# A streaming encoder layer on one core: the order of query products, scores and values on TensorE in the attention stage

## Chip, cores and metric

The kernel runs on one core of one Trainium2 chip. The metric is the device time of one execution in microseconds (us); lower is better. Timed three times it gave 2192.12 us in the median (2192.0 to 2194.67).

## What is computed

Two layers of a hybrid encoder, each over 1024 prompt rows and 8 streams of 16 rows, so 1152 rows in all (9 tiles of 128 rows; tile index 8 holds the streams). Per layer:

```
proj = rms_norm(x) @ w_in          # a, gc, gb | q (8 heads) | k, v (2 kv heads) | u, vg
y_conv = gb * conv3(gc * a)
q, k   = partial_rope(q), partial_rope(k)
p      = exp(s - m) / (sum(exp(s - m)) + exp(sink - m)),  s = q k^T / 8 over this chunk and the one before
y_attn = p v
y_gmlp = gelu(u) * (W_s layer_norm(gelu(vg)) + b)
mix    = [rms(y_conv), rms(y_attn), rms(y_gmlp)]
x      = x + mix @ w_out
x      = x + relu(rms_norm(x) @ w_ff1)^2 @ w_ff2
```

All of it is in float32. A chunk is 64 rows; in a tile of 128 prompt rows the first 64 see the chunk before and their own, the last 64 see the whole tile. The streams see the cached keys of 64 rows and their own 16.

## The kernel before

**Products.** A float32 product is made of three TensorE matmuls on split operands (high times high, high times low, low times high): `product`, lines 2131 to 2135, so "one product" below is three matmuls. `rows_by_cols` (L2140) makes the product of one tile of rows with 512 columns of weights over the given depth slices `ks`; with eight slices that is 24 matmuls. It can be called in pieces: `sum_of` says which slice starts and which ends the sum in the bank of `ps`. Weights come as units of 128x512; ScalarE rounds a unit to its high half and VectorE subtracts to get the low half (`split` on both engines).

**The attention stage.** Each engine's program is an order written out by hand, with semaphores between engines. Tile t goes through these steps:

- `rows_by_cols(..., t, U_Q, ...)` on TensorE: the queries of tile t into bank 0 of `ps` (bank 1 for index 1);
- `copy_q(t)` on ScalarE (L1168, instruction L1172): out of PSUM into `qn`, of which there is one; it also waits for the turn of t-1;
- `rotate` on VectorE (L1417, instructions L1423 to L1426): the rotary part;
- `q_turn(t)` on TensorE (L2231, instruction L2239): four 128x128 transposes into bank 2; `copy_qT(t)` on ScalarE (L1176, L1182, or L1187 for tile index 8) brings them to `qT`;
- `scores(t)` on TensorE (L2242, instructions L2259 to L2266; L2274 and L2275 for index 8) into banks 3 and 4; it waits for `copy_qT(t)` and for the exponentials of t-1, which read the same banks;
- `softmax_max(t)` on VectorE (L1483, L1489 to L1494), `exponentials(t)` on ScalarE (L1189, L1199 and L1201), `softmax_norm(t)` on VectorE (L1496, L1499 to L1501);
- `p_turn(t)` on TensorE (L2279, L2285) into banks 5 and 6; `turned_back(t)` on ScalarE (L1224, instructions L1230 and L1231) brings them to `pT` and signals `pT_done`;
- `values(t)` on TensorE (L2289, L2305, or L2311 for index 8) into bank 7; it waits for `pT_done` of t, for `value_rows(t)` on VectorE (`vmix`) and for the copy of t-1 out of bank 7;
- `mixed_high(t)`, `squares_of(t)` on ScalarE, `mixed_low(t)`, `square_sums(t)` on VectorE, and `group_sums(t)` on TensorE (L2315): the operand of the output projection and its sums of squares.

TensorE runs them as a pipeline over i = 0 to 8: `q_turn(i-1)`, queries of i, `scores(i-1)`, `values(i-3)`, `p_turn(i-2)`, `group_sums(i-4)`. ScalarE in step i runs `copy_q(i)`, `mixed_high(i-3)`, `exponentials(i-1)`, `copy_qT(i)`, `squares_of(i-3)`, `turned_back(i-2)`; in the last step (i = 8) `copy_qT(8)` comes ahead of `exponentials(7)`, and four splits of output weights lie in between. So in ScalarE's order `turned_back(6)` stands behind `exponentials(7)` and `squares_of(5)`, and behind it come four splits, `exponentials(8)`, and then for tile indices 6 and 7 `mixed_high`, `squares_of` and the next `turned_back`.

**Behind the loop** TensorE drains the pipeline while the output projection begins: `side_rows(0, t)` (L2344) makes the columns 0 to 511 of the convolution and gating part for tile t (two groups of six matmuls, in two banks), and `add_sides(0, t)` on VectorE (L1546, instruction L1543) adds both groups to `x` and so frees the banks. `side_rows(0, 1)` uses the banks of `side_rows(0, 0)` and waits for them.

**Ahead of the loop** the queries of tile index 0 and the first half of those of index 1 are already made between convolution blocks. All of it runs once in each of the two layers.

Of the kernel before, what the change touches and what calls it, by code (L numbers as in the profile page):

```python
# [46 lines left out]
TS = T - 1  # L47
ROWS = T * P
KD = D // P
# [12 lines left out]
U_KVG, U_U, U_CONV, U_Q, U_OUT, U_FF, U_END = 0, 8, 12, 24, 32, 48, 60  # L62
# [69 lines left out]
def program(nc, io, plan):  # L132
# [5 lines left out]
    with ExitStack() as ctx:  # L138
# [125 lines left out]
        ps = ctx.enter_context(nc.psum_tensor("ps", [P, 8, 512], F32))  # L264
# [82 lines left out]
        def tile(t):  # L347
            return slice(t * P, (t + 1) * P)
# [1023 lines left out]
        def _(dve):  # L1372
# [143 lines left out]
            def mixed_low(t):  # L1516
                dve.wait_ge(*mix_hi.at(t))
                for k0, k1, src in ((0, 2, yc[:, :, tile(t)]), (2, 6, yat[:]),
                                    (6, 8, ygT[:, :, tile(t)])):
                    last = V.tensor_tensor(hTl[:, k0:k1, tile(t)], src, hTh[:, k0:k1, tile(t)].bitcast(F32),  # L1520
                                           ALU.subtract)
                last.then_inc(*mix_lo.tick(t))
# [23 lines left out]
            def add_sides(n, t):  # L1546
                add_rows(n, t, 0)
                add_rows(n, t, 2)
# [257 lines left out]
            for l in range(DEPTH):  # L1806
# [42 lines left out]
                for t in range(T + LAG[l]):  # L1849
# [14 lines left out]
                    i = t - LAG[l]  # L1864
# [46 lines left out]
                for i in range(T):  # L1911
                    if i == TS:
                        split(range(U_OUT, U_OUT + 2))
                    dve.wait_ge(*qn_raw.at(i))
                    rotate(qn[:], HEADS, i, q_rot)
                    if i >= 1:
                        softmax_max(i - 1)
                    if i == TS:
                        split(range(U_OUT + 2, U_OUT + 4))
                    if i >= 2:  # L1920
                        value_rows(i - 2)
                    if i >= 3:
                        mixed_low(i - 3)
                    if i >= 1:
                        softmax_norm(i - 1)
                    if i >= 4 and i < TS:
                        group_scale(i - 4)
                    if i >= 3 and i < TS:
                        square_sums(i - 3)

                add_sides(0, 0)
                softmax_max(TS)
                group_scale(TS - 4)
                square_sums(TS - 3)
# [195 lines left out]
        def _(pe):  # L2130
# [9 lines left out]
            def rows_by_cols(out, t, first_id, ks, cols=512, sum_of=None, at=None):  # L2140

                sum_of = sum_of or ks
                for n, k in enumerate(ks):
                    i = first_id + (k if at is None else at + n)
                    if t == 0:
                        unit_ready(i)
                    s = i % 8
                    ins = product(out, hTh[:, k, tile(t)], hTl[:, k, tile(t)], wh[:, s, 0:cols], wl[:, s, 0:cols],  # L2150
                                  k == sum_of[0], k == sum_of[-1])
                    if t == TS:
                        ins.then_inc(w_used.sem, 1)
                return ins
# [87 lines left out]
            def scores(t):  # L2242


                pe.wait_ge(*qT_done.at(t))
                if t >= 1:
                    pe.wait_ge(*exp_done.at(t - 1))
                else:
                    pe.wait_ge(*kc_done.at(None))
                    pe.wait_ge(*yc_done.at((1, 2)))  # L2250
                pe.nop(nofuse=True)
                k0 = t * P
                for h in range(G4):
                    if t == TS:
                        break
                    c0 = h * P
                    sides = [(ps[:, 3 + g, :], slice(64 * g, 64 * g + 64)) for g in range(2)]
                    for bank, rows in sides:
                        pe.matmul(bank[0:64, c0:c0 + 64], qT[rows, c0:c0 + 64], kT[rows, k0:k0 + 64], start=True,  # L2259
                                  stop=True)  # L2260
                    for bank, rows in sides:
                        ins = pe.matmul(bank[64:128, c0:c0 + P], qT[rows, c0 + 64:c0 + P], kT[rows, k0:k0 + P],  # L2262
                                        start=True, stop=True)
                    if t > 0:
                        for bank, rows in sides:
                            ins = pe.matmul(bank[0:64, c0 + 64:c0 + P], qT[rows, c0:c0 + 64], kT[rows, k0 - 64:k0],  # L2266
                                            start=True, stop=True)
                if t == TS:
                    for b in range(DEC_BATCH):
                        bank = ps[:, 3 + b // 4, (b % 4) * KEYS_S:(b % 4 + 1) * KEYS_S]  # L2270
                        for g in range(2):
                            rows = slice(64 * g, 64 * g + 64)
                            qb = qT[rows, b * 64:(b + 1) * 64]
                            pe.matmul(bank[rows, 0:64], qb, kcT[rows, b * 64:(b + 1) * 64], start=True, stop=True)  # L2274
                            ins = pe.matmul(bank[rows, 64:80], qb, kT[rows, k0 + 16 * b:k0 + 16 * b + 16],  # L2275
                                            start=True, stop=True)
                ins.then_inc(*sc_full.tick(t))
# [11 lines left out]
            def values(t):  # L2289

                pe.wait_ge(*pT_done.at(t))
                if t < TS:
                    pe.wait_ge(*vmix_set.at(t))
                if t >= 1:
                    pe.wait_ge(*yat_done.at(t - 1))
                else:
                    pe.wait_ge(*zst_out.at(1))
                out = ps[:, 7, :].rearrange("p (h n) -> p h n", h=G4)
                pv = pT[:].rearrange("p (g h n) -> p g h n", g=2, h=G4)
                if t < TS:  # L2300
                    for g in range(2):
                        rows = slice(64 * g, 64 * g + 64)
                        for half, vv in enumerate((vmix[:, rows], v_sb[:, t, rows])):
                            q = slice(64 * half, 64 * half + 64)
                            ins = pe.matmul(out[rows, :, q], vv, pv[:, g, :, q], start=True, stop=True)  # L2305
                else:
                    pe.wait_ge(*vs_in.at("last"))
                    for b in range(DEC_BATCH):
                        for g in range(2):
                            rows = slice(64 * g, 64 * g + 64)  # L2310
                            ins = pe.matmul(out[rows, :, 16 * b:16 * b + 16], vs[0:KEYS_S, b, rows],  # L2311
                                            pT[0:KEYS_S, b * P + 64 * g:b * P + 64 * g + 64], start=True, stop=True)
                ins.then_inc(*pv_full.tick(t))
# [30 lines left out]
            def side_rows(n, t):  # L2344
                if n == 0:
                    pe.wait_ge(*mix_lo.at(t))
                for part, (grp, ks) in enumerate(((0, (0, 1)), (2, (6, 7)))):
                    ins = rows_by_cols(out_bank(n, t, grp), t, U_OUT + 8 * n, ks, at=2 * part)
                    if t < TS:
                        ins.then_inc(*out_full.tick((n, t, grp)))  # L2350
# [132 lines left out]
            for l in range(DEPTH):  # L2483
# [8 lines left out]
                for t in range(T + LAG[l]):  # L2492
# [15 lines left out]
                    i = t - LAG[l]  # L2508
# [46 lines left out]
                pe.wait_ge(*z_done.at((1, 1)))  # L2555
                rows_by_cols(ps[:, 1, :], 1, U_Q, range(0, 4), sum_of=range(KD))
                rows_by_cols(ps[:, 0, :], 0, U_Q, range(6, KD), sum_of=range(KD)).then_inc(*q_full.tick(0))

                for i in range(T):
                    if i >= 1:  # L2560
                        q_turn(i - 1)
                        if i >= 2:
                            pe.wait_ge(*qn_raw.at(i - 1))
                        ins = rows_by_cols(ps[:, 1 if i == 1 else 0, :], i, U_Q,
                                           list(range(KD) if i >= 2 else range(KD // 2, KD)), sum_of=range(KD))
                        if i < TS:
                            ins.then_inc(*q_full.tick(i))
                        scores(i - 1)
                    if i >= 3:
                        values(i - 3)  # L2570
                    if i >= 2:
                        p_turn(i - 2)
                    if i >= 4:
                        group_sums(i - 4)


                q_turn(TS)
                side_rows(0, 0)
                scores(TS)
                side_rows(0, 1)  # L2580
                values(TS - 2)
                p_turn(TS - 1)
                group_sums(TS - 3)
                side_rows(0, 2)
# [91 lines left out]
```

## Time and profile before

| what | value |
| --- | --- |
| median of 3 runs | 2192.12 us (2192.0 to 2194.67) |
| the profiled execution | 2193.26 us |
| its span, first to last instruction | 2191.5 us |
| TensorE busy | 2158.0 us (98%) |
| VectorE busy | 1548.0 us (71%) |
| ScalarE busy | 937.3 us (43%) |
| mean granted clock of TensorE | 0.998 of full |
| chain that ended last | PE 93%, DVE 2%, ACT 2% |

The table is of one profiled execution, but for the first line. 1.8 us of its time lie around the span. "Granted clock" is the share of 2.4 GHz that TensorE was given. PE is TensorE's matmuls, PEld its weight loads, DVE is VectorE, ACT is ScalarE. Starts are counted from the span's start. In layer 0 the attention stage lies between 194 and 305 us, in layer 1 between 1278 and 1389 us.

### The profile page before, as it was taken

What the parts mean: (1) busy time and instruction counts of PE and PEld (TensorE: products, weight loads), DVE (VectorE), ACT (ScalarE), POOL (GpSimd) and SP (SyncE); (2) the same over time, 40 slices, a digit from 0 to 9 for tenths busy, and PEclk for the clock granted to TensorE, in tenths of its full rate; (3) what the DMA queues carried; (4) which work ended last, traced back from release to release, by engine and by line L of the source; (5) the groups of instructions that cost most, each with busy time, mean ns of one, the idle gap of its engine ahead of it and who ended that gap; (6) DMA issues with size and microseconds to landing.
All of it is one profiled execution on the core that took longest, in us unless ns stands there. A gap on an engine that the chain in (4) does not pass through costs nothing.

```text
span 2191.5 us, 34116 instructions
## 1 busy us (share of the span) xinstructions
PE 2158.0 (98%) x13154; PEld 1932.4 (88%) x13154; DVE 1548.0 (71%) x2597; ACT 937.3 (43%) x1951; POOL 111.6 (5%) x205
## 2 busy tenths in 40 slices
PE   7999999999999999999999999999999999999998
PEld 5898778999999988888879987889999998888886
DVE  5524767888787787777873348578878787877768
ACT  4313833555555523233342148235555555223233
POOL 2300011000000000000022000010000000000002
PEclk9999999999999999999999999999999999999999
DMA  5211012345555786536312100223454558856363
GB/s 169 61 42 34 21 49 96 125 157 209 195 191 185 283 303 254 212 137 230 99 45 66 46 19 21 70 104 140 169 210 176 197 188 338 299 179 230 137 228 116
DMA packets 218002, 330.35 MB, mean 151 GB/s; under 512 B 14172, under 2 KB 104576, under 8 KB 217840
## 3 DMA queue, kind: packets, MB, share of 16 engines
q1 hardware_dynamic: 214768, 321.93, 41.3%
q10 hardware_dynamic: 1008, 3.67, 0.4%
q0 software_dynamic: 2064, 2.57, 0.4%
q8 instruction: 105, 1.72, 0.3%
q14 instruction: 57, 0.47, 0.1%
HBM read 212.28 MB, written 115.64 MB: 150 GB/s over the span
## 4 chain that ended last, share of the span: by engine, by line
PE 93%; DVE 2%; ACT 2%; DMA 1%; issue 1%; POOL 0%; SPq 0%; DVEq 0%; ACTq 0%; POOLq 0%
PE ps L2133 30%; PE ps L2135 29%; PE ps L2134 29%; PE ps L2177 1%; DMA w_raw<-in_w_in 1%; PE ps L2305 1%; PE ps L2285 1%; DMA ff_ops<-row_op 1%; PE ps L2227 0%; ACT S L1199 0%; PE ps L2239 0%; DVE b_all L1561 0%; PE ps L2262 0%; PE ps L2259 0%; ACT q L927 0%
## 5 line engine op out<-in xcount | busy, mean ns | idle before, releaser
L2133 PE MATMUL ps<-h_all,w_hi 128*128 128x288 f32 (+1 forms) x1504 | 471.2, 313 | 0.9 <-DVE q L1695 0.9
L2135 PE MATMUL ps<-h_all,w_lo 128*128 128x288 f32 (+1 forms) x1504 | 470.2, 313 | 0.0
L2134 PE MATMUL ps<-h_all,w_hi 128*128 128x288 f32 (+1 forms) x1504 | 469.5, 312 | 0.0
L2133 PEld LDWEIGHTS ps<-h_all,w_hi 128*128 128x128 f32 x1504 | 282.2, 188 | 2.9 <-DVE q L1695 1.3
L2134 PEld LDWEIGHTS ps<-h_all,w_hi 128*128 128x128 f32 x1504 | 282.2, 188 | 0.1
L2135 PEld LDWEIGHTS ps<-h_all,w_lo 128*128 128x128 f32 x1504 | 282.2, 188 | 0.0
L2133 PE MATMUL ps<-w_hi,h_all 128*128 128x512 f32 x576 | 232.3, 403 | 2.9 <-DVE w_lo L1387 1.7
L2135 PE MATMUL ps<-w_hi,h_all 128*128 128x512 f32 x576 | 226.1, 393 | 0.0
L2134 PE MATMUL ps<-w_lo,h_all 128*128 128x512 f32 x576 | 226.0, 392 | 0.0
L2133 PE MATMUL ps<-w_hi,ring_all 128*128 128x512 f32 x544 | 211.6, 389 | 0.0
L2134 PE MATMUL ps<-w_lo,ring_all 128*128 128x512 f32 x544 | 211.6, 389 | 0.0
L2135 PE MATMUL ps<-w_hi,ring_all 128*128 128x512 f32 x544 | 211.6, 389 | 0.0
L2135 PE MATMUL ps<-s,w_lo 128*128 128x288 f32 x624 | 184.2, 295 | 0.0
L2134 PE MATMUL ps<-s,w_hi 128*128 128x288 f32 x624 | 183.7, 294 | 0.0
L2133 PE MATMUL ps<-s,w_hi 128*128 128x288 f32 x624 | 183.5, 294 | 0.0
L2133 PE MATMUL ps<-w_hi,ring 128*128 128x512 f32 x448 | 174.8, 390 | 0.3 <-DVE x L1781 0.3
L2135 PE MATMUL ps<-w_hi,ring 128*128 128x512 f32 x448 | 174.4, 389 | 0.0
L2134 PE MATMUL ps<-w_lo,ring 128*128 128x512 f32 x448 | 174.3, 389 | 0.0
L983 ACT ACTIVATE w_hi<-b_all 128x512 fp32r<-128x512 f32 x128 | 70.3, 621 | 237.6 <-PE ps L2135 174.1
L1006 ACT ACTIVATE w_hi<-w_raw 128x512 fp32r<-128x512 f32 x182 | 110.4, 624 | 111.7 <-DVE w_raw L1629 40.9
L983 ACT ACTIVATE w_hi<-w_raw 128x512 fp32r<-128x512 f32 x96 | 56.6, 629 | 186.9 <-DVE w_raw L1733 96.7
L2133 PEld LDWEIGHTS ps<-w_hi,h_all 128*128 128x128 f32 x576 | 109.1, 189 | 27.8 <-DVE w_lo L1387 3.2
(247 smaller groups left out, 4082.9 us busy)
## 6 DMA issues: line engine op xcount, KB each, us to landing
ff_ops<-row_op SPq DMA_DIRECT2D x128, 512.0 KB, 3.3
w_raw<-in_w_ff SPq DMA_DIRECT2D x128, 256.0 KB, 3.5
ring_all<-ff_ops SPq DMA_DIRECT2D x32, 1024.0 KB, 8.3
ring<-ff_ops SPq DMA_DIRECT2D x32, 1024.0 KB, 8.4
ff_raw<-q SPq DMA_DIRECT2D x96, 256.0 KB, 3.4
b_all<-in_w_ff SPq DMA_DIRECT2D x24, 1024.0 KB, 12.1
w_raw<-in_w_in SPq DMA_DIRECT2D x64, 256.0 KB, 3.4
ring<-ff_raw SPq DMA_DIRECT2D x12, 1024.0 KB, 5.6
```

The source lines that it names most:

```text
L983: nc.scalar.activation(wh[:, HALF * half + j, :], w[:, j, :], ACT.Copy).then_inc(op_hi, 1)
L1006: nc.scalar.activation(wh[:, fslot(b, i), :], raw[:, FRAW[kind], :], ACT.Copy).then_inc(f_hi, 1)
L2133: pe.matmul(out, sh, mh, start=first, stop=False)
L2134: pe.matmul(out, sh, ml, start=False, stop=False)
L2135: return pe.matmul(out, sl, mh, start=False, stop=last)
L2177: ins = pe.transpose(ps[:, bank, (k % 4) * P:(k % 4 + 1) * P], xn[:, t % 2, tile(k)], ident[:])
L2285: ins = pe.transpose(ps[0:n, 5 + h // 4, (h % 4) * P:(h % 4 + 1) * P], S[:, t % 2, h * n:(h + 1) * n], ident[:])
L2305: ins = pe.matmul(out[rows, :, q], vv, pv[:, g, :, q], start=True, stop=True)
```

## The change

On TensorE the second half of the queries of tile index 1 moves ahead of the loop, that is ahead of `q_turn(0)`. In step i = 1 there are then two of the eight depth slices of tile index 2 between `q_turn(0)` and `scores(0)`, and step i = 2 makes the other six. Behind the loop `values(6)` (`values(TS - 2)`, the seventh tile) moves from behind `side_rows(0, 1)` to ahead of `scores(8)`. On VectorE `add_sides(0, 0)` moves from behind the loop into step i = 8, ahead of `softmax_norm(7)`. ScalarE's order, the DMA queues and GpSimd are left as they are; no instruction is added or taken away.

```diff
@@ VectorE, in step i @@
                     if i >= 3:
                         mixed_low(i - 3)
+                    if i == TS:
+                        add_sides(0, 0)
                     if i >= 1:
                         softmax_norm(i - 1)
@@ VectorE, behind the loop @@
-                add_sides(0, 0)
                 softmax_max(TS)
@@ TensorE @@
                 rows_by_cols(ps[:, 0, :], 0, U_Q, range(6, KD), sum_of=range(KD)).then_inc(*q_full.tick(0))
+                rows_by_cols(ps[:, 1, :], 1, U_Q, range(4, KD), sum_of=range(KD)).then_inc(*q_full.tick(1))
 
                 for i in range(T):
                     if i >= 1:
                         q_turn(i - 1)
-                        if i >= 2:
-                            pe.wait_ge(*qn_raw.at(i - 1))
-                        ins = rows_by_cols(ps[:, 1 if i == 1 else 0, :], i, U_Q,
-                                           list(range(KD) if i >= 2 else range(KD // 2, KD)), sum_of=range(KD))
-                        if i < TS:
-                            ins.then_inc(*q_full.tick(i))
+                        if i == 1:
+                            pe.wait_ge(*qn_raw.at(0))
+                            rows_by_cols(ps[:, 0, :], 2, U_Q, range(0, 2), sum_of=range(KD))
+                        else:
+                            if i >= 3:
+                                pe.wait_ge(*qn_raw.at(i - 1))
+                            ins = rows_by_cols(ps[:, 0, :], i, U_Q, range(2 if i == 2 else 0, KD), sum_of=range(KD))
+                            if i < TS:
+                                ins.then_inc(*q_full.tick(i))
                         scores(i - 1)
@@ TensorE, behind the loop @@
                 q_turn(TS)
                 side_rows(0, 0)
+                values(TS - 2)
                 scores(TS)
                 side_rows(0, 1)
-                values(TS - 2)
                 p_turn(TS - 1)
```

## Rows read from the trace of the kernel before

**Rows 1.** The page: busy time, share of the span and instructions of each engine
```profile
PE 2158.0 (98%) x13154; PEld 1932.4 (88%) x13154; DVE 1548.0 (71%) x2597; ACT 937.3 (43%) x1951; POOL 111.6 (5%) x205
```

**Rows 2.** Waits of PE, whole span: total us, times, longest us
```profile
PE ps L2239 <- DVE qn L1426: 4.7, 4, 1.7
PE ps L2274 <- issue: 1.8, 2, 0.9
...
PE ps L2133 <- DVE x L1543: 0.7, 2, 0.4
```

**Rows 3.** Timeline of PE, layer 0, start of the loop: start us, us, idle before
```profile
193.80 0.39 PE L2135 MATMUL ps<-w_hi,h_all 128*128 128x512 f32 x1
195.87 0.66 PE L2239 MATMUL ps<-ident,qn 128*128 128x128 f32 x4 [1.68 <-DVE qn L1426]
196.28 0.48 PE L2133 MATMUL ps<-w_hi,h_all 128*128 128x512 f32 x1
...
199.21 0.27 PE L2259 MATMUL ps<-kT,qT 64*64 64x64 f32 x2
...
200.96 0.66 PE L2239 MATMUL ps<-ident,qn 128*128 128x128 f32 x4 [0.65 <-DVE qn L1426]
...
207.00 0.27 PE L2259 MATMUL ps<-kT,qT 64*64 64x64 f32 x2
...
208.09 1.09 PE L2285 MATMUL ps<-ident,S 128*128 128x128 f32 x8
```

**Rows 4.** Timeline of ACT, same stretch
```profile
196.56 0.60 ACT L1182 ACTIVATE qT<-ps 128x512 f32<-128x512 f32 x1 [1.74 <-PE ps L2239]
199.32 0.60 ACT L1172 ACTIVATE qn<-ps 128x512 f32<-128x512 f32 x1 [2.16 <-PE ps L2135]
...
206.18 0.64 ACT L1182 ACTIVATE qT<-ps 128x512 f32<-128x512 f32 x1
```

**Rows 5.** Timeline of DVE, same stretch
```profile
200.02 0.29 DVE L1423 TENSOR_TENSOR rtA<-qn,cosb 128x128 f32<-128x128 f32 x1 [4.21 <-ACT qn L1172]
...
200.61 0.29 DVE L1426 TENSOR_TENSOR qn<-rtA,rtB 128x128 f32<-128x128 f32 x1
201.08 0.48 DVE L1489 MEMSET ps<- 64x512 f32 x1 [0.17 <-DVE qn L1426]
...
206.80 1.22 DVE L1501 TENSOR_TENSOR S<-S,den 128x1024 f32<-128x1024 f32 x1
```

**Rows 6.** Timeline of PE, layer 0, behind the loop
```profile
269.12 0.39 PE L2135 MATMUL ps<-w_hi,h_all 128*128 128x512 f32 x1
270.40 0.34 PE L2274 MATMUL ps<-kcT,qT 64*64 64x64 f32 x4 [0.89 <-issue]
...
272.80 0.58 PE L2133 MATMUL ps<-w_hi,h_all 128*128 128x512 f32 x1 [0.35 <-DVE x L1543]
...
277.32 0.66 PE L2305 MATMUL ps<-pT,vmix 128*64 128x256 f32 x4
...
278.35 1.09 PE L2285 MATMUL ps<-ident,S 128*128 128x128 f32 x8
...
285.48 0.66 PE L2305 MATMUL ps<-pT,vmix 128*64 128x256 f32 x4
```

**Rows 7.** Timeline of ACT, same stretch
```profile
270.04 0.25 ACT L1201 ACTIVATE es<-sd 128x8 f32<-128x8 f32 x1
...
271.75 0.65 ACT L1231 ACTIVATE pT<-ps 128x512 f32<-128x512 f32 x1
...
281.71 0.59 ACT L1231 ACTIVATE pT<-ps 128x512 f32<-128x512 f32 x1
```

**Rows 8.** Timeline of DVE, same stretch: the sides of tile index 0
```profile
271.91 1.63 DVE L1543 SCALAR_TENSOR_TENSOR x<-ps,rG,x 128x512 f32<-128x512 f32 x2
```

**Rows 9.** Busy time in two stretches: PE, PEld, DVE, ACT, POOL (instructions), granted clock, DMA
```profile
272.80:277.32 4.52, 4.52 (x12) 3.31 (x12) 3.77 (x13) 4.52 (x21) 0.85 (x1) 0.62 0.00 0
1357.10:1360.00 2.90, 2.90 (x12) 2.14 (x12) 2.82 (x11) 2.90 (x11) 0.69 (x1) 1.00 0.00 0
```

## The prediction

> **What bounds the kernel now.** I read the page first: TensorE is busy for 98% of the span, VectorE for 71%, ScalarE for 43% [rows 1]. So no engine but TensorE matters on average, and a change that only reorders work can gain no more than the time in which TensorE stands still where the change is made. The table of waits says how much that is [rows 2]: TensorE waits four times for the rotated queries (4.7 us), twice ahead of the streams' scores (1.8 us) and twice for the banks of the first side products (0.7 us), 7.2 us in all over both layers. The timelines of layer 0 place them: 1.68 us ahead of the first turn, 0.65 us ahead of the second [rows 3], 0.89 and 0.35 us behind the loop [rows 6]. That makes 3.57 us in a layer, and layer 1 repeats it. All the rest of the stage has no gap on TensorE.
>
> The row of 0.89 us names "issue" as its releaser, which is to be read with care: `scores(8)` waits for the exponentials of index 7, and the last of these ends at 270.04 + 0.25 = 270.29 [rows 7], 0.11 us ahead of the start at 270.40 [rows 6]. I take 0.1 us as the way from ScalarE's end to TensorE's start below.
>
> **Part 1, the queries ahead.** Twelve matmuls of 512 columns move ahead of `q_turn(0)`, six of tile index 2 take their place. The pace of such matmuls comes from the timeline [rows 3]: the twelve between 196.28 and the scores at 199.21 took 2.93 us with the change to scores included; the 24 from 200.96 + 0.41 = 201.37 to 207.00 took 5.63, so twelve more cost 2.70 and one 0.225 us. (0.41 is the step from the turn at 195.87 to the next product at 196.28.)
>
> Now step by step, in times of layer 0. The last product ahead of the loop starts at 193.80 and hands over at 194.03. Twelve more end at 196.75; with 0.1 for the change of operand the first turn starts at 196.85. The queries are rotated well before that (the turn could start at 195.87), so the 1.68 us are filled. Products of index 2 start at 197.26; six take 2.93 - 6 x 0.225 = 1.58, so `scores(0)` starts at 198.84 instead of 199.21. Its `qT` copy moves with the turn from 196.56 to 197.54 and ends at 198.14 [rows 4], in time. Before, the scores ended at 200.96 - 0.65 = 200.31, 1.10 us after their start; now at 199.94. `copy_q(1)` needs the turn of index 0 and follows the `qT` copy in ScalarE's order: 198.14 to 198.74 instead of 199.32 to 199.92 [rows 4]; the rotation (200.02 to 200.90, so 0.98 us behind the copy) [rows 5] ends at 199.72. So `q_turn(1)` finds its data when `scores(0)` is through, at some 199.9, and the 0.65 us are filled too.
>
> **What is late next.** `softmax_max(0)` on VectorE starts when the scores are there, at 199.97 instead of 201.08 [rows 5]: 1.1 us earlier, and no more, since 0.4 us come from the scores and the rest from the rotation that no longer stands ahead of it. From there the chain is as before: maxima, eight exponentials, the `qT` copy of index 1 behind them in ScalarE's order (206.18, now 205.07, ending at 205.71) [rows 4], and `scores(1)`, which needs that copy. It was ready at 206.82, and TensorE came at 207.00 [rows 3]: nearly even. Now TensorE is through with the 18 remaining matmuls at 199.9 + 0.41 + (5.63 - 6 x 0.225) = 204.6, and can start at 205.8. A new wait of 1.2 us stands there. `p_turn(0)` needs the normalised S: 206.80 + 1.22 = 208.02 [rows 5], and ran at 208.09 [rows 3]; now 1.1 us earlier, right behind `scores(1)`. From there on everything is shifted by 1.1 us and nothing else. Gain of part 1: 1.1 us in a layer, not the 2.3 of the filled gaps. Bounds: no gain at all if another step of the first iterations proves tight, and 2.3.
>
> **Part 2, values ahead of the streams' scores.** `values(6)` needs `pT_done` of 6, that is `turned_back(6)` on ScalarE, which stands behind `exponentials(7)` and `squares_of(5)`. It ends at 271.75 + 0.65 = 272.40 [rows 7]. The side products end their issue at 269.12 + 0.23 = 269.35 [rows 6]. So TensorE would stand from there to 272.50, some 3 us, in place of the 0.89; ScalarE's program isn't changed and has no gap there, so `pT_done` doesn't come sooner against TensorE. Behind the waiting `values(6)` are queued `scores(8)`, whose own wait ends at 270.40, and everything after. The values take 278.35 - 277.32 = 1.03 us [rows 6], so `scores(8)` starts at 273.53; it takes 272.80 - 0.35 - 270.40 = 2.05, so `side_rows(0, 1)` starts at 275.58. Before, it started at 272.80 with the values still ahead of it, comparable to 273.83. Loss: 1.75 us in a layer. In the changed order the second gap (0.35) has gone, that is in this sum. Bounds: the loss can't be below 1.6 unless ScalarE is early, nor much above 2.
>
> Who waits for the later scores: `softmax_max(8)`, `exponentials(8)` start some 2.2 us later (the scores end at 275.58 instead of 272.45, ScalarE was still splitting weights). Behind them stands `turned_back(7)`, which ended at 281.71 + 0.59 = 282.30 against `values(7)` at 285.48 [rows 6, 7]: 3.2 us of cover, and TensorE comes later as well. I cost it at nothing; without this cover it would be up to 2 us.
>
> **Part 3, the adds.** Two instructions of 1.63 us together [rows 8] move ahead of `softmax_norm(7)`. They need side products that are out at 269.51 [rows 6] and free the banks before TensorE asks for them. `softmax_norm(7)` is then ready by some 273.2, and its reader `p_turn(7)` comes behind 278: nothing.
>
> **The clock.** Two stretches set side by side show one more thing [rows 9]: the twelve matmuls behind `scores(8)` took 4.52 us in layer 0, the same twelve 2.90 in layer 1. The granted clock was 0.62 in the mean of the first stretch and 1.00 in the second: TensorE had fallen to its lower level, 1.2 GHz, after the gap of 0.89, the small matmuls of the streams' scores and the gap of 0.35, and it cost 1.62 us. In layer 1 the same quiet stretch didn't bring it down. The change makes this stretch longer: 3.1 us standing, 1.03 of values, 2.05 of scores. I expect a fall in both layers more often than not, but part of the low clock then falls on the standing and on the scores, whose many small matmuls may be limited by their weight loads rather than by the array. The price per layer lies between 0 and 1.62 twice over; I take 1.0. The Trainium skill (TensorE: Matmul & The Clock Gate, Part 1) has the rule that the gate gives the full clock only to an engine kept busy and takes it back from a quiet one, and its advice is against gaps between bursts of matmuls. By that rule the change pays in both layers, which is rival (c) below with 2196.6; by the trace, one quiet stretch in two fell.
>
> **Sum.** Per layer -1.1 + 1.75 = +0.65, for both +1.3, and +2.0 for the clock. The profiled execution took 2193.26 us (span 2191.5 and 1.8 around it) and holds one fall of the clock for 1.62; without it it would be 2191.6. The median of the three runs, 2192.12, lies between, nearer to the one without a fall, and I count from it: 2192.1 + 1.3 + 2.0 = 2195.4. A difference under 0.2% (4.4 us) can't be told from none here, so this is no measurable change, on the slow side.
>
> **Rivals.** (a) All gaps go. For it: each edit lies at one of the four. It needs `turned_back(6)` ahead of 269.4 and the exponentials of index 0 about 1.2 us sooner, against [rows 4, 7]. It would give 2 x 3.57 = 7.1 less: 2185, and 2183.5 if no fall of the clock is left. (b) Front works, tail is neutral: 2190. It needs only `turned_back(6)` at some 270.7; nothing in ScalarE's order allows it. (c) Slower beyond 0.2%, by the clock. The 3.1 us wait plus scores bring TensorE to 1.2 GHz in both layers, and the time at that level falls on the side products behind, as in [rows 9], once or longer. Price 1.62 each for one such stretch: 2192.1 + 1.3 + 3.2 = 2196.6; at twice the length 2199.9. It decides from 1.6 us a layer on. For it: the fall after a shorter quiet stretch in layer 0. Against: none in layer 1, nor in the loop, where products follow. (d) The new wait ahead of `scores(1)` is followed by a low clock in the first iterations, and the 2.2 us of part 1 go: 2197.6. The gap of 1.68 had no fall behind it, since twelve matmuls took 2.93 us there [rows 3], so this is unlikely.
>
> **Chances.** My forecast with its variants of the clock below 1.6 a layer: 0.65. (c): 0.24. (d): 0.04. (b): 0.04. (a): 0.03. (b) counts as no change. The forecast's own range is from 2192.3 (front a bit better, no fall) to 2196.5. The range reaches into (c) and a little below: 2191.5 to 2198.0. Faster 0.04, within 0.2% 0.69, slower 0.27.
>
> **What would show it.** Waits of TensorE: L2239 gone from the list; a wait of about 1.2 us ahead of the scores of index 1 (L2259) released by the `qT` copy L1182; ahead of `values(6)` (L2305) about 3 us released by ScalarE's L1231, once per layer; none at L2274 and none for L1543. The turn of index 0 at 196.9, `p_turn(0)` at 207.0. In windows behind the streams' scores, granted clock below 1 in one or both layers. I would be wrong if the values start near 268.6 without a wait, if `scores(1)` start below 205, or if there is a third wait in the loop that I don't list.

## The result, and the profile after

| | kernel before | changed kernel |
| --- | --- | --- |
| median | 2193.22 us (14 runs, 2191.16 to 2195.82) | 2198.75 us (14 runs, 2195.18 to 2202.58) |
| profiled execution | 2193.26 us | 2200.82 us |
| its span | 2191.5 us | 2199.0 us |
| mean granted clock | 0.998 | 0.995 |

The ratio is 1.0024, 95% interval 1.0017 to 1.0031: slower by some 5.5 us. The forecast was 2195.4 with a range to 2198.0, so it had the right side and too little of it. 1.1 us of the miss is the base (the kernel before gave 2192.12 in its first three runs, 2193.22 in fourteen).

The time of the changed kernel follows its granted clock from run to run: the one run with a mean of 0.998 took 2195.18 us, the one with 0.994 took 2202.58, and the other twelve lie between them in the order of their clock. The profiled execution, at 0.995, is the second longest of the fourteen, so the profile shows more time at the low clock than the median run had.

The page of the changed kernel, its span and first lines; these answer to [rows 1]:

```profile
span 2199.0 us, 34116 instructions
...
PE 2163.7 (98%) x13154; PEld 1937.7 (88%) x13154; DVE 1548.2 (70%) x2597; ACT 937.1 (43%) x1951; POOL 111.5 (5%) x205
```

TensorE has the same 13154 matmuls and is busy 5.7 us longer. Waiting alone can't do that: some matmuls ran slower. TensorE's lines are moved by one from here on (L2133 is L2134 in the changed kernel, and so on); ScalarE's keep their numbers.

Waits of TensorE over the whole span, two rows that answer to [rows 2]:

```profile
PE ps L2306 <- ACT pT L1231: 5.9, 2, 2.9
PE ps L2260 <- ACT qT L1182: 2.9, 2, 1.4
```

All three old rows are gone, as the four gaps were filled. Two new ones stand in their place, 8.8 us in all against 7.2: `values(6)` waits 2.9 us for ScalarE's `turned_back`, and `scores(1)` waits 1.4 us for the `qT` copy, each once per layer.

TensorE's timeline at the start of the loop in layer 0, against [rows 3]. The first row is the last thing of the convolution, which stood at 188.23 before, so 0.36 us of each start came from further ahead:

```profile
188.59 0.27 PE L2209 MATMUL ps<-ident,zT 128*2 128x128 f32 x1
...
197.11 0.60 PE L2240 MATMUL ps<-ident,qn 128*128 128x128 f32 x4
...
199.04 0.27 PE L2260 MATMUL ps<-kT,qT 64*64 64x64 f32 x2
...
200.07 0.66 PE L2240 MATMUL ps<-ident,qn 128*128 128x128 f32 x4
...
206.28 0.27 PE L2260 MATMUL ps<-kT,qT 64*64 64x64 f32 x2 [1.43 <-ACT qT L1182]
...
207.40 1.09 PE L2286 MATMUL ps<-ident,S 128*128 128x128 f32 x8
```

The `qT` copy that released `scores(1)`, in ScalarE's timeline, against [rows 4]:

```profile
205.50 0.63 ACT L1182 ACTIVATE qT<-ps 128x512 f32<-128x512 f32 x1
```

Both turns start without a wait. `p_turn(0)` starts 18.81 us behind the last row of the convolution, 19.86 before: 1.05 us are gained, of 2.33 in the two gaps; the new wait of 1.43 takes back the rest.

TensorE behind the loop, against [rows 6]:

```profile
268.39 0.39 PE L2136 MATMUL ps<-w_hi,h_all 128*128 128x512 f32 x1
271.71 0.82 PE L2306 MATMUL ps<-pT,vmix 128*64 128x256 f32 x4 [2.93 <-ACT pT L1231]
...
273.31 0.49 PE L2275 MATMUL ps<-kcT,qT 64*64 64x64 f32 x4
...
276.87 0.79 PE L2134 MATMUL ps<-w_hi,h_all 128*128 128x512 f32 x1
...
280.65 1.03 PE L2286 MATMUL ps<-ident,S 128*128 128x128 f32 x8
```

and the copy that released the values, in ScalarE's timeline, against [rows 7]:

```profile
271.02 0.64 ACT L1231 ACTIVATE pT<-ps 128x512 f32<-128x512 f32 x1
```

The wait is where it was forecast: the copy ends at 271.66, 0.74 us earlier than before, about the 1.05 gained at the start of the loop less the 0.36 from further ahead. The values start 0.05 us behind it. What follows takes longer than the same work took before. Stretches of the changed kernel (PE, PEld, DVE, ACT, POOL, granted clock, DMA): first values, scores and side products of layer 0, then the same of layer 1.

```profile
271.71:273.31 1.60, 1.59 (x8) 0.61 (x8) 0.72 (x1) 1.60 (x3) 0.00 (x0) 0.62 0.00 0
273.31:276.87 3.56, 3.56 (x67) 3.52 (x65) 0.00 (x0) 0.79 (x2) 0.00 (x0) 0.50 0.00 0
276.87:280.65 3.78, 3.78 (x14) 3.02 (x13) 3.16 (x12) 2.33 (x15) 0.85 (x1) 0.73 0.02 4
...
1358.43:1360.35 1.92, 1.92 (x9) 0.79 (x9) 0.72 (x1) 1.92 (x4) 0.00 (x0) 0.50 0.04 9
1360.35:1363.90 3.55, 3.55 (x67) 3.51 (x65) 0.00 (x0) 0.47 (x1) 0.00 (x0) 0.50 0.00 0
1363.90:1368.54 4.64, 4.64 (x15) 3.65 (x13) 3.23 (x12) 3.19 (x19) 0.85 (x1) 0.58 0.00 0
```

All of the scores ran at 0.50, that is 1.2 GHz, and took 3.56 us where they had taken 2.05 [rows 6]. The two stretches at the low level as wholes:

```profile
272.10:278.90 6.80, 6.80 (x77) 5.45 (x74) 2.18 (x11) 2.58 (x8) 0.34 (x1) 0.50 0.00 0
1357.50:1367.80 10.30, 9.37 (x81) 7.43 (x82) 4.81 (x16) 5.77 (x23) 0.85 (x1) 0.50 0.01 2
```

Before, the profiled execution had one such stretch in its tails, of 3.4 us (0.62 in the mean of 4.52 us), in layer 0, and none in layer 1 [rows 9].

### The profile page after: what moved, and what is told of

Read it like the earlier page. It is cut to its first block, busy times and chain, and to the rows that moved or that the text cites. A ratio compares the mean times of both kernels' runs of the same rounds, so it can differ in the third digit from the quotient of the medians.

```text
span 2199.0 us, 34116 instructions
## 1 busy us (share of the span) xinstructions
PE 2163.7 (98%) x13154; PEld 1937.7 (88%) x13154; DVE 1548.2 (70%) x2597; ACT 937.1 (43%) x1951; POOL 111.5 (5%) x205
## 4 chain that ended last, share of the span: by engine, by line
PE 92%; DVE 2%; ACT 2%; DMA 1%; issue 1%; SPq 0%; POOL 0%; DVEq 0%; ACTq 0%; POOLq 0%
PE ps L2134 29%; PE ps L2136 29%; PE ps L2135 29%; PE ps L2178 1%; DMA w_raw<-in_w_in 1%; PE ps L2306 1%; ACT S L1199 1%; PE ps L2286 1%; DMA ff_ops<-row_op 0%; PE ps L2228 0%; PE ps L2240 0%; PE ps L2263 0%; PE ps L2260 0%; DVE b_all L1561 0%; PE ps L2275 0%
## 5 line engine op out<-in xcount | busy, mean ns | idle before, releaser
L2134 PE MATMUL ps<-h_all,w_hi 128*128 128x288 f32 (+1 forms) x1504 | 471.2, 313 | 0.9 <-DVE q L1695 0.9
L2134 PEld LDWEIGHTS ps<-h_all,w_hi 128*128 128x128 f32 x1504 | 282.2, 188 | 2.7 <-DVE q L1695 1.3
L2134 PE MATMUL ps<-w_hi,h_all 128*128 128x512 f32 x576 | 233.5, 405 | 1.4 <-DVE h_all L1412 0.9
L2134 PE MATMUL ps<-w_hi,ring_all 128*128 128x512 f32 x544 | 211.6, 389 | 0.0
L2134 PE MATMUL ps<-s,w_hi 128*128 128x288 f32 x624 | 183.5, 294 | 0.0
L2134 PE MATMUL ps<-w_hi,ring 128*128 128x512 f32 x448 | 174.7, 390 | 1.0 <-DVE x L1781 1.0
L2134 PEld LDWEIGHTS ps<-w_hi,h_all 128*128 128x128 f32 x576 | 109.6, 190 | 26.7 <-DVE w_lo L1387 2.2
```

The lines of the kernel that those rows point to most:

```text
L2134: pe.matmul(out, sh, mh, start=first, stop=False)
```

## The experiments

Three theories were set against each other. **A**: the queries gain some 1.05 us a layer; the tail loses by its wait and by the low clock behind it. **B**: the new wait ahead of `scores(1)` eats the gain of the queries. **C**: the tail's loss beyond its wait isn't the clock, but something that comes late behind the later scores. Each kernel was timed together with the kernel before on the same chip; differences are between medians of runs taken together. e1 to e4 ran on one chip, e5 to e8 on a second, e9 to e11 on a third, so kernels of different groups are compared only through the kernel before.

| kernel | median us | before | difference | 95% interval of the ratio |
| --- | --- | --- | --- | --- |
| e1 queries alone | 2190.09 | 2192.22 | -2.13 | 0.9983 to 1.0000 |
| e2 tail alone | 2199.70 | 2192.22 | +7.48 | 1.0016 to 1.0039 |
| e3 queries and adds | 2189.46 | 2192.22 | -2.76 | 0.9977 to 0.9995 |
| e4 changed, wait filled | 2193.64 | 2192.22 | +1.42 | 0.9995 to 1.0013 |
| e5 changed, ScalarE's order | 2188.42 | 2192.49 | -4.07 | 0.9971 to 0.9990 |
| e6 e3, queries balanced | 2187.17 | 2192.49 | -5.32 | 0.9965 to 0.9985 |
| e7 e3, side products split | 2188.35 | 2192.49 | -4.14 | 0.9969 to 0.9987 |
| e8 e6 and e7 | 2186.00 | 2192.49 | -6.49 | 0.9956 to 0.9981 |
| e9 before, gap filled | 2192.07 | 2191.59 | +0.48 | 0.9992 to 1.0010 |
| e10 changed, wait half filled | 2193.85 | 2191.59 | +2.26 | 1.0003 to 1.0021 |

The profiles give a second measure, free of the spread of the runs: the time on TensorE from the last row of the convolution to the start of `p_turn(7)`, in layer 0. It needs the granted clock to stay at 1.00, as it did in this stretch in all of these but layer 0 of the kernel before.

| kernel | us from the convolution's end to `p_turn(7)` |
| --- | --- |
| before | 90.12 in layer 0, with 1.62 for its low clock; 88.52 in layer 1 |
| e1, e3 | 87.43, 87.08 |
| e4, e10 | 89.06, 89.07 |
| e5, e6 | 86.92, 86.19 |
| e7, e8 | 86.44, 85.61 |
| e9 | 88.50 |

**e1, the queries alone.** The changed kernel with the tail put back:

```diff
                 side_rows(0, 0)
-                values(TS - 2)
                 scores(TS)
                 side_rows(0, 1)
+                values(TS - 2)
```

and `add_sides(0, 0)` behind VectorE's loop again.

> Only the queries ahead of the loop; values of index 6 and the adds as before. Theory A (the queries gain 1.05 us a layer, the whole loss is the tail): 2.1 us below the kernel before, and in the profile p_turn of index 0 some 1.05 us earlier against the last product of the convolution. Rival B (the new wait of 1.4 us ahead of the scores of index 1 costs what the filled gaps give): within 0.5 us of the kernel before.

2.13 us below the kernel before. Waits of TensorE in e1, whole span:

```profile
PE ps L2259 <- ACT qT L1182: 2.9, 2, 1.4
PE ps L2274 <- issue: 1.8, 2, 0.9
```

The wait of 1.4 is there in full, and the gain of 1.05 a layer beside it: in e1's profile too `p_turn(0)` starts 18.81 us behind the last row of the convolution, 19.86 before. The interval of the times reaches 1.0000, so the times of e1 alone would only make the gain likely; with the profile, B falls.

**e2, the tail alone.** The kernel before with the values and the adds moved as in the change, the queries untouched.

> Only the values of index 6 ahead of the streams' scores, and the adds earlier; queries as before. Theory A: the changed kernel's 5.5 us and the 2.1 us of the queries that are missing here, some 7.6 us above the kernel before. Rival B: 5.5 us above. Both expect a wait of 2.9 us for ScalarE's turned_back of index 6 in each layer.

7.48 us above, with waits of 2.9 us in both layers, and in its profile low clocks of 6.8 and 10.2 us as in the changed kernel. e1 and e2 together make +5.35, the change +5.53: the parts add up to within the noise, and the tail is all of the loss.

**e3, queries and adds.** As e1, but with the adds where the change has them.

> Queries ahead and the adds of index 0 ahead of softmax_norm(7), but values of index 6 where they were. Theory A: the wait of 0.35 us for the first banks goes as well, 2 x (1.05 + 0.35) = 2.8 us below the kernel before, perhaps more where the clock doesn't fall any more. Rival B: 0.7 us below. If the adds cost something by standing ahead of softmax_norm(7), it is not below the kernel with the queries alone.

2.76 below, of 2.8 expected. The wait of 0.35 is gone. Against e1, run on the same chip, it is 0.63 us, less than the runs of either kernel spread, so the times alone don't show that the adds gain. The profiles do: 0.35 us in layer 0, the wait that is gone. And the mean clock is 0.999 in all eleven runs of e3, while three of the eleven of e1 list 0.998 and are 2.7 us longer in the mean; that the second gap helps to bring the clock down is likely from this, and not shown.

**e4, the wait filled.** The changed kernel with this ahead of `values(TS - 2)`, so TensorE is not left standing:

```diff
                 side_rows(0, 0)
+                pe.wait_ge(*yat_done.at(TS - 3))
+                for n in range(4):
+                    k = n
+                    product(ps[:, 7, :], hTh[:, k, tile(0)], hTl[:, k, tile(0)], wh[:, 0, :], wl[:, 0, :], n == 0,
+                            n == 3)
                 values(TS - 2)
```

> The changed kernel with twelve more matmuls of 512 columns (2.7 us, their result is overwritten and unused) in bank 7, ahead of values(6), where TensorE otherwise waits 2.9 us. Theory A (the wait costs 1.75 us a layer, the rest of the loss is the clock at 1.2 GHz behind it): granted clock 1.00 throughout the tail, values(6) still at the time of turned_back(6), and 4.5 to 6 us below the changed kernel although it does more. Rival C (the rest of the loss is something that comes late behind the later scores, not the clock): the same as the changed kernel or above it.

1.42 above the kernel before, where the changed kernel is 5.5 above: there are 24 more matmuls of 512 columns, over both layers, whose result nobody reads, and the time is some 4.1 us less. Filler, values, scores and side products of layer 0:

```profile
268.50:271.39 2.89, 2.66 (x13) 1.88 (x11) 2.69 (x7) 2.89 (x11) 0.00 (x0) 1.00 0.47 138
271.39:272.41 1.02, 1.02 (x9) 0.50 (x9) 0.69 (x1) 1.02 (x3) 0.00 (x0) 1.00 0.00 0
272.41:274.40 1.99, 1.99 (x66) 1.96 (x65) 0.00 (x0) 1.36 (x3) 0.00 (x0) 1.00 0.00 0
274.40:277.26 2.86, 2.86 (x16) 2.31 (x13) 2.64 (x12) 1.41 (x9) 0.85 (x1) 1.00 0.03 6
```

`values(6)` still start with `turned_back(6)`: 83.19 us behind the last row of the convolution, 83.12 in the changed kernel. So what hangs on late values and scores gets them no sooner but by the clock, which is 1.00 throughout. C falls. From the convolution to `p_turn(7)` a layer of e4 takes 0.54 us more than layer 1 of the kernel before, 1.1 in both: that is what the change costs with the clock held up. From these rows the price of the clock can be read: values, scores and side products take 1.02 + 1.99 + 2.86 = 5.87 us here, 1.60 + 3.56 + 3.78 = 8.94 in layer 0 of the changed kernel and 1.92 + 3.55 + 4.64 = 10.11 in layer 1. That is 3.1 and 4.2 us for the low level, 7.3 in the profiled execution; the medians, with 4.1, say less, since most runs had a higher mean clock than the profiled one.

**e5, ScalarE's order.** The changed kernel, and on ScalarE in the last step:

```diff
                         copy_qT(TS)
+                        turned_back(TS - 2)
                     if i >= 1:
                         exponentials(i - 1)
...
-                    if i >= 2:
+                    if i >= 2 and i < TS:
                         turned_back(i - 2)
```

> The changed kernel with one move on ScalarE: turned_back(6) ahead of exponentials(7) in the last step. Theory A (the tail loses because values(6) stand in TensorE's queue ahead of a copy that ScalarE's order makes late): the wait of 2.9 us ahead of values(6) goes, one of about 1 us ahead of the streams' scores comes back, since the exponentials of index 7 end 1 us later, and the clock falls rarely: 8 to 9.5 us below the changed kernel, level with the kernel with queries and adds alone. Rival (values(6) are costly in that place whatever ScalarE does): at most 3 us below the changed kernel.

4.07 below the kernel before, so 9.6 below the changed one (8 to 9.5 expected). It was expected level with e3: the medians put it 1.3 below, the profiles 0.16 a layer. TensorE in e5, layer 0 (lines moved by two):

```profile
268.41 0.66 PE L2307 MATMUL ps<-pT,vmix 128*64 128x256 f32 x4
...
270.34 0.34 PE L2276 MATMUL ps<-kcT,qT 64*64 64x64 f32 x4 [0.84 <-issue]
...
272.32 0.50 PE L2135 MATMUL ps<-w_hi,h_all 128*128 128x512 f32 x1
...
275.19 1.03 PE L2287 MATMUL ps<-ident,S 128*128 128x128 f32 x8
```

ScalarE in e5, the copy moved ahead:

```profile
266.75 0.61 ACT L1231 ACTIVATE pT<-ps 128x512 f32<-128x512 f32 x1
```

The operand of the values is there at 267.36 instead of 271.66, and the values no longer wait. What is wrong with the change is thus not the place of the values in TensorE's order, but that its counterpart on ScalarE stayed behind 3 us of `exponentials(7)` and 1.1 us of `squares_of(5)`. The gap of 0.84 ahead of the scores is the old one of 0.89: the values come before it and don't fill it, since the exponentials of index 7 are later by the copy. They end at 270.25, 0.09 us ahead of the scores, which bears out that the releaser called "issue" is this wait.

**e6, the queries balanced.** As e3, and:

```diff
-                rows_by_cols(ps[:, 1, :], 1, U_Q, range(4, KD), sum_of=range(KD)).then_inc(*q_full.tick(1))
+                rows_by_cols(ps[:, 1, :], 1, U_Q, range(4, 7), sum_of=range(KD))
...
                         q_turn(i - 1)
                         if i == 1:
-                            pe.wait_ge(*qn_raw.at(0))
-                            rows_by_cols(ps[:, 0, :], 2, U_Q, range(0, 2), sum_of=range(KD))
+                            rows_by_cols(ps[:, 1, :], 1, U_Q, range(7, KD), sum_of=range(KD)).then_inc(*q_full.tick(1))
...
                         scores(i - 1)
+                        if i == 1:
+                            pe.wait_ge(*qn_raw.at(0))
+                            rows_by_cols(ps[:, 0, :], 2, U_Q, range(0, 2), sum_of=range(KD))
```

> The kernel of queries and adds alone, with the queries split otherwise: three of the four depth slices of index 1 ahead of the first turn, the fourth between first turn and first scores, and the two slices of index 2 behind the first scores instead of ahead of them. Theory A: the chain from the first scores over maxima and exponentials to the qT copy of index 1 sets the start of scores(1), so what counts is how soon the first scores start; here they start some 1.2 us earlier against the convolution's last product, the rotation of index 1 then takes back part of it, the wait of 1.4 us shrinks to 0.4 to 0.9: 1 to 1.5 us below the kernel of queries and adds over both layers. Rival: it is the amount of products between the turns that counts; no difference.

TensorE in e6, layer 0:

```profile
196.19 0.60 PE L2240 MATMUL ps<-ident,qn 128*128 128x128 f32 x4
...
197.56 0.27 PE L2260 MATMUL ps<-kT,qT 64*64 64x64 f32 x2
...
200.09 0.60 PE L2240 MATMUL ps<-ident,qn 128*128 128x128 f32 x4
...
205.18 0.27 PE L2260 MATMUL ps<-kT,qT 64*64 64x64 f32 x2 [0.36 <-ACT qT L1182]
```

The first scores start at 197.56 instead of 199.04 and the new wait shrinks from 1.43 to 0.36, with the same products in all: the chain through the first scores, not the amount of products, sets `scores(1)`. e6 is 5.32 below the kernel before. Against e3 that is 2.6 by the medians and 0.89 a layer, 1.8 in all, by the profiles, more than the 1 to 1.5 expected.

**e7 and e8.** e7 is e3 with the first six matmuls of `side_rows(0, 1)` ahead of the streams' scores, and VectorE's first add ahead of `mixed_low(5)` (VectorE's lines and the body of `side_part` aren't shown):

```diff
                 side_rows(0, 0)
+                side_part(0, 1, 0)
                 scores(TS)
-                side_rows(0, 1)
+                side_part(0, 1, 1)
                 values(TS - 2)
```

> The kernel of queries and adds alone, with the first six matmuls of side_rows(0, 1) ahead of the streams' scores and VectorE's first add of index 0 ahead of mixed_low(5). It fills the 0.9 us ahead of the scores with work that is ready. Theory A with the clock: 0.9 us a layer less and no quiet stretch long enough for a fall, so 1.8 us or more below the kernel of queries and adds, and a spread of runs narrower than that of the kernel before. Rival: the first add comes too late and the 0.9 us only move: no difference.

> Both of the last two changes together. If they are independent, the sum: 3 to 3.5 us below the kernel of queries and adds alone, 6 us below the kernel before. Rival: the shifts meet in ScalarE's order and one of the gains is lost.

e7 is 4.14 below the kernel before, e8 6.49 below, at 2186.0 us the fastest of all: e7 and e6 gain on e3 1.4 and 2.6 us by these differences, and e8 3.7, near their sum. By the profiles it is 0.64 and 0.89 us a layer, and 1.47 for e8. e7 stays under the 1.8 that was expected of it. e8's largest wait in the stage is 0.4 us per layer:

```profile
PE ps L2262 <- ACT qT L1182: 0.7, 2, 0.4
```

**e9, the gap of the kernel before filled.** Three matmuls, as in e4 with `range(1)`, ahead of `scores(TS)` in the kernel before.

> The kernel before with three more matmuls of 512 columns (0.7 us, unused result in bank 7) in the gap of 0.9 us ahead of the streams' scores. Theory: the spread of the kernel before (2190 to 2196 us) is the clock falling in the tail in some runs and layers; with the quiet stretch shorter it falls rarely, so the same work plus nothing gives a median 0.5 to 1.5 us lower and a narrower spread. Rival: the spread is something else; the median is the same or up to 0.5 us higher.

0.48 above, with an interval that holds 1, so no difference; 0.5 to 1.5 less was expected. The runs spread from 2190.8 to 2193.4, those of the kernel before, run beside it, from 2190.5 to 2193.7. The gain that the theory promised didn't come, but this doesn't clear the clock. On this chip there was little to win: only 2 of 21 runs of the kernel before list a mean clock of 0.998 instead of 0.999, and none of e9. Over the three chips 18 of 73 runs of the kernel before list 0.998, and on each chip these are in the mean 1.4 to 1.9 us longer than the others there, close to the 1.62 of one fall [rows 9]. So falls of the clock in some runs are likely a part of the spread; no profile shows where they lie. The runs at 0.999 alone still reach from 2190.1 to 2194.1, and what spreads those stays open.

**e10 and e11.** e10 is e4 with `range(2)`: six matmuls.

> The changed kernel with six more matmuls (1.4 us) in the wait of 2.9 us ahead of values(6), half of the filling that kept the clock up. What stands still is then 1.5 us, followed by values and scores. If the low clock needs a standing engine for most of it, the clock stays up and the time is that of the fully filled kernel, 5 us below the changed one; if the small matmuls of values and scores count as quiet too, it still falls in some runs, and the time lies 2 to 4 us below the changed kernel with a wide spread.

Waits of TensorE in layer 0 of e10:

```profile
PE ps L2306 <- ACT pT L1231: 1.6, 1, 1.6
```

Eight of its eleven runs lie between 2192.2 and 2194.2 us, three between 2196.2 and 2197.4. The eight list a mean clock of 0.999, the three 0.997. In the profile, one of the eight, the clock stays at 1.00 in both tails, and the time to `p_turn(7)` is that of e4. Half of the filling is thus enough in most runs; the three others are 3.2 us longer in the mean, which fits a fall in one layer at the 3.1 to 4.2 us read above, though no profile of them was taken.

> The changed kernel once more, for a second profile. The two waits of 1.4 and 2.9 us per layer come out the same to 0.1 us; the time at the low clock in the tails may differ from the 6.8 and 10.3 us of the first profile, and the span differs by what the clock does and by nothing else.

e11 took 2199.97 us, with the same waits. Its two stretches at the low level:

```profile
270.50:280.80 10.30, 9.54 (x82) 7.50 (x83) 4.65 (x14) 5.78 (x24) 0.85 (x1) 0.50 0.01 3
1359.40:1366.30 6.90, 6.90 (x76) 5.64 (x73) 2.45 (x12) 2.91 (x10) 0.85 (x1) 0.51 0.01 2
```

The long and the short one have changed places: 10.3 us in layer 0 and 6.9 in layer 1. With e2, three profiles of this tail show a fall in both layers, one of some 6.8 and one of some 10.3 us, and which of the layers has the long one changes. Whether it is so in every run isn't shown: the fourteen runs of the changed kernel list mean clocks from 0.994 to 0.998.

## Why the prediction was right or wrong

**What bounds.** Right: the four gaps, 7.2 us, were what an order could win. The best order, e8, got 6.5 of them. One remark beside it was wrong: that a difference under 4.4 us can't be told from none. The interval of fourteen runs is 0.07% to each side, 1.5 us, and would have shown the forecast 3.3.

**Part 1.** Right, step by step: first turn at 196.85 plus the 0.36 of this execution (197.11 seen), `scores(0)` at 198.84 (199.04 seen), `scores(1)` at 205.8 plus 0.36 (206.28 seen), a new wait of 1.2 (1.4 seen), a gain of 1.1 a layer (1.05 in the profile, 2.13 for both in e1). Rival (d), a low clock behind that wait, didn't come: no profile shows one at the start of the loop.

**Part 2.** Right: 3 us standing ahead of `values(6)`, released by ScalarE's L1231 (2.9 seen). With the clock held up, in e4, the whole change costs 1.42 us in the medians and 1.1 in the profiles, against 1.3 in the sum. The cover of `turned_back(7)` held; no further wait appeared.

**Part 3.** Right: no cost, and the wait of 0.35 gone.

**The clock: here the prediction failed.** The mechanism was named; the term was sized too small. The prediction took "1.0" per layer out of a range of "between 0 and 1.62 twice over". From e2 (+7.48) and the wait of 1.75 a layer the clock took 4.0 us for both layers in the median, not 2.0; in the profile 3.1 and 4.2, the second beyond the range. The reason for taking little was that the low level would fall on the standing "and on the scores", whose many matmuls "may be limited by their weight loads rather than by the array". They took 3.56 us at the low level and 1.99 at the full one. So a low clock under the scores costs 1.6 us, as much as the fall under the side products cost in [rows 9]. Nor did much of it fall on the standing: nothing in layer 0, 0.9 us in layer 1. And the low stretch was not of the one length that [rows 9] showed, but two and three times it. Rival (c) was the case that came; it had 0.24. The median, 2198.75, lies between its two prices, 2196.6 and 2199.9, nearer to the second. With 4.0 for 2.0 and the base of the fourteen runs the sum gives 2193.2 + 1.3 + 4.0 = 2198.5. That it comes so near says that the parts add up, as the 4.0 is itself worked out from a measured time.

The rule of the Trainium skill that the prediction weighed (TensorE: Matmul & The Clock Gate, Part 1: full clock only for an engine kept busy) was right for both layers in both profiles of the changed kernel, with 6.8 to 10.3 us at 1.2 GHz. The prediction set one fall in two from the kernel before against it. That evidence was taken for more than it was, since the quiet stretch there had half the length: 3.3 us of gaps and scores, against 2.9 standing and 3.0 of values and scores at the full clock (e4) in the changed order.

## What to carry to other kernels

Moving work ahead on one engine's queue is only half of an edit: look up where the producer of its operand stands in the other engine's queue, and move that too (e5 turned +5.5 us into -4.1 with one call). Filling a gap moves the bound to the next link, so order for the chain that runs through the gap's end, and not by the amount of work that fits (e6). And price a wait of TensorE of some 3 us with light work behind it at more than its length: here 1.75 us of delay brought 2 us more by the clock, which goes where the gap is filled with products, even with such as nobody needs (e4).

## What was not expected of the hardware

- The fall outlasts its cause. In the changed kernel's first profile the engine fell to 1.2 GHz at 272.1 in layer 0, when it had stood for 2.9 us and had just begun the values, and at 1357.5 in layer 1, still standing; it rose at 278.9 and 1367.8, both times when side products had run for 2.0 and 3.9 us. In no profile did it rise during the scores. In all three profiles of this tail (changed kernel, e2, e11) the long stretch, 10.2 to 10.3 us, was the one that had begun while TensorE still stood, 2.0 to 2.2 us into the wait, and the short one, 6.8 to 6.9 us, had begun when the matmuls ran again. What decides between the two isn't shown.
- Values and scores with only 0.2 us standing ahead of them didn't bring the clock down in the profile of e4, nor did they in e5, with 0.84 us ahead of the scores, or, in most runs, with 1.6 us ahead of the values (e10). But in layer 0 of the kernel before gaps of 0.89 and 0.35 us around the scores did, and in layer 1 the same gaps did not, so the length of the quiet stretch alone did not decide it.
- The streams' scores, 32 float32 matmuls per layer on 64x64 operands with 64 or 16 columns, take 3.56 us at the low level and 1.99 at the full one, a ratio of 1.8, though each is tiny.
